# Block compression of a sparse-attention layer: convolution over token pairs in split fp32r, and another order of the dense products

## What is computed

```python
def compress(k_all, pe, w1, w2):
    L = k_all.shape[1]
    n_cmp = (L - CMP_BLOCK) // CMP_STRIDE + 1          # block 32, stride 16
    idx = jnp.arange(n_cmp)[:, None] * CMP_STRIDE + jnp.arange(CMP_BLOCK)[None, :]
    blocks = k_all[:, idx] + pe[None, None, :, None, :]
    hid = jax.nn.gelu(jnp.einsum('bnjgd,jde->bnge', blocks, w1))
    return jnp.einsum('bnge,ef->bngf', hid, w2)
```

## Time and profile before

| | |
|---|---|
| median of 3 runs | 1938.66 us (1932.65 to 1939.78) |
| profiled execution | 1939.67 us, its span 1938.0 us |
| mean granted TensorE clock | 0.918 |
| TensorE / VectorE / ScalarE / GpSimd busy | 1732.1 / 737.3 / 632.9 / 221.3 us |
| compression stage in the trace | 969.8 to 1077.9 us |
| DMA, whole run | 133.47 MB, mean 69 GB/s |

### The profile page before, as it was taken

How to read it: one execution, slowest core, us unless ns; L and a number is a source line. 1 busy time by engine, 2 the same in 40 slices (tenths; PEclk the granted TensorE clock), 3 DMA queues, 4 the chain that set the end, 5 groups by cost and what they waited for, 6 DMA issues and landing times. The chain is left out here.

```text
span 1938.0 us, 31215 instructions
## 1 busy us (share of the span) xinstructions
PE 1732.1 (89%) x12354; PEld 1535.7 (79%) x12354; DVE 737.3 (38%) x1422; ACT 632.9 (33%) x1256; POOL 221.3 (11%) x310
## 2 busy tenths in 40 slices
PE   8994398799999999799779799999697999999996
PEld 7993268699999899699634567767485999998994
DVE  4326953533333222454222354344445333332224
ACT  4425352422222111454112354454314222221113
POOL 1003521200000000100100233232011000000000
PEclk9997698899999999799879679899787999999997
DMA  5322002122222332233452100000321322223321
GB/s 152 90 75 61 22 19 70 44 87 87 87 87 87 90 90 60 44 77 98 113 153 33 44 20 26 1 1 1 110 66 44 87 87 87 87 87 90 90 60 46
DMA packets 257289, 133.47 MB, mean 69 GB/s; under 512 B 47191, under 2 KB 256619, under 8 KB 257003
## 3 DMA queue, kind: packets, MB, share of 16 engines
q1 hardware_dynamic: 247754, 128.44, 23.8%
q10 hardware_dynamic: 8832, 2.20, 0.8%
q0 software_dynamic: 608, 1.57, 0.3%
HBM read 125.88 MB, written 10.43 MB: 70 GB/s over the span
## 5 line engine op out<-in xcount | busy, mean ns | idle before, releaser
L211 PE MATMUL ps<-x_hi,w_hi 128*128 128x272 f32 x2288 | 662.5, 290 | 4.6 <-DVEq L574 4.2
L213 PE MATMUL ps<-x_hi,w_lo 128*128 128x272 f32 x2288 | 664.3, 290 | 0.0
L212 PE MATMUL ps<-x_lo,w_hi 128*128 128x272 f32 x2288 | 659.7, 288 | 0.0
L211 PEld LDWEIGHTS ps<-x_hi,w_hi 128*128 128x128 f32 x2288 | 432.7, 189 | 6.5 <-DVEq L574 4.8
L212 PEld LDWEIGHTS ps<-x_lo,w_hi 128*128 128x128 f32 x2288 | 433.1, 189 | 0.0
L213 PEld LDWEIGHTS ps<-x_hi,w_lo 128*128 128x128 f32 x2288 | 431.8, 189 | 0.0
L226 DVE TENSOR_TENSOR w_lo<-w_raw,w_hi 128x1024 fp32r<-128x1024 f32 (+1 forms) x167 | 226.2, 1355 | 492.5 <-ACT w_hi L219 492.5
L219 ACT ACTIVATE w_hi<-w_raw 128x1024 fp32r<-128x1024 f32 (+1 forms) x179 | 199.6, 1115 | 643.2 <-PE ps L213 636.3
L211 PE MATMUL ps<-h_hi,w_hi 128*128 128x272 f32 x704 | 204.7, 291 | 9.6 <-DVEq L784 9.6
L213 PE MATMUL ps<-h_hi,w_lo 128*128 128x272 f32 x704 | 204.7, 291 | 0.0
L212 PE MATMUL ps<-h_lo,w_hi 128*128 128x272 f32 x704 | 204.4, 290 | 0.0
(11 more groups left out here) (371 smaller groups left out, 2079.2 us busy)
## 6 DMA issues: line engine op xcount, KB each, us to landing
w_raw<-in_ffn_w_gate SPq DMA_DIRECT2D x44, 512.0 KB, 3.9
w_raw<-in_ffn_w_up SPq DMA_DIRECT2D x44, 512.0 KB, 3.9
w_raw<-in_ffn_w_down SPq DMA_DIRECT2D x32, 704.0 KB, 4.6
w_raw<-in_ab_w_in SPq DMA_DIRECT2D x17, 512.0 KB, 4.2
w_raw<-in_c_w_in SPq DMA_DIRECT2D x13, 512.0 KB, 3.8
w_raw<-in_c_w_in SPq DMA_DIRECT2D x16, 256.0 KB, 3.8
w_raw<-in_c_w_out SPq DMA_DIRECT2D x32, 128.0 KB, 3.0
w_raw<-in_ab_w_in SPq DMA_DIRECT2D x10, 256.0 KB, 4.6
```

Of the source, the lines that this page charges most:

```text
L211: pe.matmul(out, c.w_hi[:, slot, k, :], x_hi[:, k0 + k, cols], start=first, stop=False)
L212: pe.matmul(out, c.w_hi[:, slot, k, :], x_lo[:, k0 + k, cols], start=False, stop=False)
L213: last = pe.matmul(out, c.w_lo[:, slot, k, :], x_hi[:, k0 + k, cols], start=False, stop=end)
```

## The change

1. **Token pairs.** A row of the line is now a pair of tokens: partitions are 2 tokens x 64 channels of one head, columns are the pairs, kept in 8 phases (a block is 16 pairs, the stride 8). The DMA brings a pair into one partition: a slot of 128 x 512 holds two pages (64 pairs each), filled by four DMAs of 256-byte pieces. One transpose per head gives the line directly.
2. **Tap halves side by side.** The 128 output columns of a weight tile are taps 0 to 15 and taps 16 to 31 of the same pair position, 64 channels each. One product gives both halves; the second half, shifted by one block, is added afterwards (`shift` on ScalarE, `add` on VectorE). No zeros stand in the weights.
3. **Split fp32r.** Weights and line are split into high and low parts: ScalarE copies, VectorE subtracts. Eight phases x 3 products x 2 column cuts (322 and 320) are 48 matmuls a tag.
4. Weights, position rows and `w2` are loaded by GpSimd in the row stage, with the pairs of the first four sequences; SP loads the other twelve in the compression stage, into 8 slots. Each pair's load reads its page numbers again.
5. The two window copies move into `fetch_values`, at the end of SP's loads in the prompt attention.
6. `pe_unit` goes through both column halves for each row tile.

```diff
 def pe_unit(c, pe, slot, kt, k0, x_hi, x_lo, bank, start, stop):
-    for h in range(2):
-        cols = slice(h * HALF, (h + 1) * HALF)
-        out = c.ps[:, bank + h, 0:HALF]
-        for k in range(kt):
-            first, end = start and k == 0, stop and k == kt - 1
+    halves_of = [(c.ps[:, bank + h, 0:HALF], slice(h * HALF, (h + 1) * HALF)) for h in range(2)]
+    for k in range(kt):
+        first, end = start and k == 0, stop and k == kt - 1
+        for out, cols in halves_of:
             pe.matmul(out, c.w_hi[:, slot, k, :], x_hi[:, k0 + k, cols], start=first, stop=False)
+        for out, cols in halves_of:
             pe.matmul(out, c.w_hi[:, slot, k, :], x_lo[:, k0 + k, cols], start=False, stop=False)
+        for out, cols in halves_of:
             last = pe.matmul(out, c.w_lo[:, slot, k, :], x_hi[:, k0 + k, cols], start=False, stop=end)
...
+def fetch_pair(c, eng, table, step, slot, tags=("k", "v")):
...
+    for g in range(NPAGE):
+        page = page_number(eng, table, b * NPAGE + g, cache)
+        for par in range(2):
+            yield eng.dma_start(slot[HD * g:HD * g + HD, :].rearrange("p (g two e) -> p two g e", two=2, g=4)[:, par],
+                                cache[0][bass.ds(page, 1)].rearrange("a (p two) g e -> p two (a g) e", two=2)[:, par])
...
             @blk.tensor
             def _(pe):
+                pe.transpose(pe_cols, pe_rows[:, :], c.k("ident")[0:2 * PAIRS, 0:2 * PAIRS]).then_inc(pe_t, 1)
                 for tag in range(2):
+                    for n in range(tag * DEC_B, (tag + 1) * DEC_B):
                         if n >= 4:
+                            m = n - 4
+                            pe.wait_ge(line_lo_set, m // DEC_B * n_line + 5 + m % DEC_B + 1)
...
+                        for s in range(2):
+                            for a in range(2):
+                                o, g = (2 * s + a) * P, (2 * a + s) * P
+                                last = pe.transpose(T_BANK(n)[:, o:o + P], slots[n % n_ring][:, g:g + P], c.k("ident"))
                         last.then_inc(turned, 1)
+                    if tag:
                         second(pe, 0)
...
+                    for f in range(PHASES):
+                        at = slice(f * P, (f + 1) * P)
+                        for w, x in ((w_hi, x_hi), (w_hi, x_lo), (w_lo, x_hi)):
+                            for i, (a, b) in enumerate(cuts):
+                                last = pe.matmul(c.ps[:, i, 0:b - a], w[tag][:, at], x[:, f, a:b],
+                                                 start=f == 0 and w is w_hi and x is x_hi, stop=f == PHASES - 1 and w is w_lo)
                     last.then_inc(hid, 1)
...
+                def shift(tag):
+                    act.wait_ge(hid, tag + 1)
...
+                    for i, (a, b) in enumerate(cuts):
+                        copy(h_shift[:, a:b - 1], c.ps[HD:P, i, 1:b - a]).then_inc(shifted, 1)
...
+                for tag in range(2):
+                    w_high(tag)
+                    if tag:
+                        shift(0)
+                    else:
+                        act.wait_ge(pe_t, 1)
+                    copy(pe_of(x_hi), pe_src(tag)).then_inc(line_hi_set, 1)
+                    for s, par in quarters:
+                        copy(prompt_of(x_hi, s, par), prompt_src(tag, s, par)).then_inc(line_hi_set, 1)
+                    for b in range(DEC_B):
+                        n = tag * DEC_B + b
+                        if tag and b == 4:
+                            activate(0)
+                        act.wait_ge(turned, n + 1)
+                        copy(tile_of(x_hi, b), turned_of(n)).then_inc(line_hi_set, 1)
+                    stacks.fill_hi(copy, stacked, tag * n_hi // 2, (tag + 1) * n_hi // 2)
+                shift(1)
+                activate(1)
...
             def fetch_pages(pool, sem):
...
-                for n in range(RING_C):
...
-                pool.wait_ge(landed, 16 * RING_C)
+                raw, _, _ = compress_weights(c)
+                for tag, name in enumerate("kv"):
+                    pool.dma_start(raw[tag].rearrange("p (j e) -> p j e", e=HD), d["c_cmp_w1_" + name][0]
+                                   .rearrange("(j two) d e -> (two d) j e", two=2)).then_inc(landed, 16)
+                for n in range(n_early):
+                    for load in fetch_pair(c, pool, table, (0, n), page_slots[n]):
+                        load.then_inc(landed, 16)
+                zeroed = sem("w2_zeroed")
+                pool.memset(w2d[:, :, :], 0.0).then_inc(zeroed, 1)
+                pool.wait_ge(zeroed, 1)
...
+                pool.wait_ge(landed, 16 * (2 + 4 * n_early + 6))
```

More of the change, by code:

```diff
@@ L1800, in stage_compress @@
+    cuts = [(0, CUT), (CUT, COLS)]
+    h_shift, h_sum = w_raw[0][0:HD, 0:COLS], w_raw[0][HD:P, 0:COLS]
+    n_line = 1 + 4 + DEC_B
     with ExitStack() as tmp:
         sb = lambda n, s, dt=F32: tmp.enter_context(nc.sbuf_tensor(n, s, dt))
[L1802 to L1805, removed]
+        x_hi = sb("cp_line_hi", [P, PHASES, COLS], F32R)
+        x_lo = sb("cp_line_lo", [P, PHASES, COLS], F32R)
@@ new lines, in prompt_src, with pe_of, pe_src, _ @@
+        def prompt_src(tag, s, par):
+            slab = (8, 14)[tag]
+            return projT[rows_of(s), slab:slab + 2, 0:SEQ].rearrange("p a (n f two) -> p two f a n", f=PHASES, two=2)[:, par]
+        def pe_of(x):
+            return x[:, :, PE0:PE0 + 2]
+        def pe_src(tag):
+            return pe_cols[:, tag * PAIRS:(tag + 1) * PAIRS].rearrange("p (h f) -> p f h", h=2)
+        quarters = [(s, par) for s in range(2) for par in range(2)]
+        with block as blk:
+            @blk.sync
+            def _(sp):
+                for n in range(n_early, len(steps)):
+                    if n >= n_ring:
+                        sp.wait_ge(turned, n - n_ring + 1)
+                    for page in fetch_pair(c, sp, table, steps[n], slots[n % n_ring]):
+                        page.then_inc(land[n % n_ring], 16)
@@ L1809, in _ @@
             @blk.gpsimd
             def _(pool):
[L1811 to L1836, removed]
@@ L1873, in _ @@
[L1873 to L1876, removed]
+                    pe.wait_ge(w_lo_set, tag + 1)
+                    pe.wait_ge(line_lo_set, (tag + 1) * n_line)
+                    if tag:
+                        pe.wait_ge(summed, 2)
@@ L1878, in _ @@
                 second(pe, 1)
[L1880 to L1887, removed]
             n_hi, n_lo = len(stacks.hi), len(stacks.lo)
@@ L1925, in _, with w_high @@
-                for tag in range(2):
-                    if tag:
-                        act.wait_ge(hid, 1)
-                    else:
-                        act.wait_ge(zeroed, 3)
-                    load_w1(tag)
-                    if not tag:
-                        for i in range(2):
-                            for s in range(2):
-                                own = rows_of(s)
-                                act.dma_start(w2d[own, i, own], d["c_cmp_w2_" + tags[i]][0]).then_inc(small_in, 16)
-                                act.dma_start(rows[:, i, own], d["c_cmp_pe_" + tags[i]][0]).then_inc(small_in, 16)
-                    place(act, copy, tag, 1)
-                    for n in range(tag * per + 1, (tag + 1) * per, 2):
-                        move(act, copy, n)
-                    stacks.fill_hi(copy, stacked, tag * n_hi // 2, (tag + 1) * n_hi // 2)
-                    act.wait_ge(hid, tag + 1)
-                    copy(bias[:, tag:tag + 1], c.ps[:, 0, N:N + 1]).then_inc(bias_m, 1)
-                    act.wait_ge(bias_m, tag + 1)
+                def w_high(tag):
+                    copy(w_hi[tag].rearrange("p (f h e) -> p f h e", h=2, e=HD), by_phase(w_raw[tag])).then_inc(w_hi_set, 1)
```

134 lines of the change are left out of this document (84 added, 50 removed).

## The result

The changed kernel takes **1890.12 us** (median of 4 runs, 1887.53 to 1896.29) against 1938.84 (median of 4, 1932.65 to 1939.78) for the kernel before beside it: a ratio of 0.976, 95% interval 0.9729 to 0.9791. The forecast was 1907, the range 1882 to 1930.

A forecast was written before the change was run, and what follows sets the result against it. TensorE was taken to bound both convolutions, ScalarE and VectorE the stretch between. Against the profiled 1939.67 us, -46.3 (compression stage) and +13 (row stage) gave -33, so 1907 us; range 1882 to 1930.

The forecast's parts named there:

- the attention's clock: Attention behind the compression stage: up to 18 us either way if another phase wakes the clock earlier or later.
- The bound now: Compression stage before the change: TensorE bounds both convolutions, ScalarE and VectorE the stretch between them.
- Part 1: Convolution: 48 matmuls a tag, 9.2 us with a slow clock start; ends 7.0 (full clock) and 12.8 us.
- Part 2: Feeding the convolutions: SP's issuing decides, 3.3 us a pair (2.8 to 4.0); stage 61.8 us, 46.3 less.
- Part 3: Loads moved to GpSimd in the row stage: +13 us, ends +6 and +31.
- the nearest rival: Row stage: pieces cost GpSimd nothing, issue stays 0.54 us; +6 instead of +13, total 1900 us; 25%.
- the 1900 rival: Row stage: GpSimd's issue stays 0.54 us whatever the size, +6 us, total 1900 us; 25%.
- The slower rival: Row stage: making descriptors on GpSimd costs 11 ns a piece, +78 us, total 1971 us; 11%.
- Part 4: Dense products' new order over 8,976 matmuls: 0 us taken, from -9 to +18.
- the rival at 1 to 2 ns: Dense products: the new order costs 1 to 2 ns a matmul, 9 to 18 us more, total 1920; 5%.
- the one at -12: Dense products: the new order saves up to 12 ns a matmul, 108 us less, total 1800; 5%.
- Part 5: Window copies moved to SP's queue in the prompt attention: cost nothing; without that cover 28 us.

The follow-up runs named there:

- two queues: Changed kernel with every second page pair of the compression stage fetched by GpSimd instead of SP: 1865.69 us, ratio 0.9659.
- the run with the late second product: Changed kernel with odd page pairs fetched by GpSimd, and the keys' GELU and second product moved behind the values' tiles: 1877.99 us, ratio 0.9731.
- the changed kernel's second trace: Changed kernel run again without edit, beside the kernel before: 1899.86 us, ratio 0.9822.
- fillers: Two 512-column products added before each of the attention's first ten wide score tiles: changed kernel 1888.91 us, kernel before 1925.37, changed with odd pairs on GpSimd 1873.38.

## Why the prediction was right, and which terms were off

The sign, the bound and the order of the parts held; the forecast was 17 us too high. Of these, 15 are the attention's clock, 9 the row stage and 5 the dense order, and 12 go the other way, in the stage. The number owes something to luck, twice over. The forecast of -33 is close to the 35 us of the change itself because three misses, +12, -9 and -5, nearly cancel. And the 49 us between the first medians came of a draw: the four runs of before lay at 1932 to 1940 us where later ones went down to 1923.5, and the changed kernel's trace met the short attention.

**The bound now: right.** TensorE bound both convolutions, and with them gone it waits for landed pairs.

**Part 1: right.** 9.2 us a convolution, measured 8.7 and 8.6. The choice was whether it starts slow. TensorE's timeline in the first one, two products to a line:

```profile
995.82 0.73 PE L1917 MATMUL ps<-cp_line_hi,x_hi 128*128 128x322 f32 x2
996.36 0.74 PE L1917 MATMUL ps<-cp_line_lo,x_hi 128*128 128x322 f32 x2
...
999.80 0.47 PE L1917 MATMUL ps<-cp_line_hi,x_lo 128*128 128x322 f32 x2
1000.10 0.46 PE L1917 MATMUL ps<-cp_line_hi,x_hi 128*128 128x322 f32 x2
```

0.27 us a product up to 997.4, the level of 1.2 GHz, then 0.15, that of 2.4 GHz. It rose after some 3.3 us where the earlier trace rows took 4.7, hence 8.7. The Trainium skill's rule ("TensorE: Matmul & The Clock Gate", Part 4) that transposes don't count for the clock as products do agrees with both of these starts, and with the earlier trace rows it doesn't: there the clock rose at 989.8 with nothing but transposes running (0.50 up to 989.7, 1.00 from 989.8), and the first convolution ran at 1.00. With two queues the second convolution ran at 1.00 from its start too, in 7.3 us, near my lower price of 7.0, and in the run with the late second product it started slow and took 10.1. So the rule is no certainty here; both prices occur.

**Part 2: the mechanism right, the size off.** SP decides, as said, and the pair costs 4.3 us, above even my high end of 4.0. The term that was mis-sized is the price of a DMA on SP: I took 0.34 to 0.43 from loads of another shape, though I had 0.6 in Part 3 for the same half-page load on GpSimd; SP takes 0.598. A page number costs about 0.95 where I had 0.74. Twelve pairs by 1.0 us are 12, and the stage was 12.2 longer than forecast. The second convolution starts 56.5 us into the stage, not 43.5. The other terms held: landing 2.3 (2.0), tail 9.0 (9.1). One that I had wrong cost nothing: the four copies of the prompt's columns on ScalarE take 4.4 us, not 2.2, and end long before the pages have landed.

**Part 3: the nearest rival's price.** +4.2, where the flat price gave +6 and I took +13. "Sixteen times the pieces must cost something" was right and small: 0.6 us more for 1,792 more pieces, 0.3 ns each, against the 4.2 ns of my upper bound. The flat 0.54 to 0.58 of the earlier trace rows was the better guide, and the 1900 rival had this term right. The rule of the Trainium skill ("DMA: Bandwidth & Descriptors", Anatomy of one DMA), that many descriptors can be emitted before the incremental cost shows, agrees with these rows up to 256 pieces a DMA (0.60 and 0.62 us); at 2,048 the cost shows, 1.2 us. The slower rival, 11 ns a piece, is excluded by the same row.

**Part 4: nearly right.** The dense order is worth -5 us, inside -9 to +18. A matmul in the new order, which changes bank each time, comes 0.6 ns cheaper; neither the rival at 1 to 2 ns nor the one at -12 holds.

**Part 5: right.** The window copies cost nothing in either place.

**The attention's clock: the bound was right, and it fell on one side.** I had allowed 18 us either way and put half into the range. It gave 14.8. That it fell on the good side was chance: the changed kernel's second trace gave 333.8, 0.8 more than before. My condition ("if another phase wakes the clock") fits the two groups of traces, 6.0 to 6.8 us and 8.2 to 8.5 us behind the fall; that the phase is the cause isn't shown.

## What to carry to other kernels

Price a fetch of small tiles by the DMA and its address arithmetic, on the queue and in the form in which it will be issued, and count them: here 48 DMAs at 0.6 us and their page numbers set the stage once the arithmetic was cheap, and a second issuing engine was worth 20 us of stage, more than half of the 34 that the rewrite had brought there. Before a difference is given to a change, cut both traces at the same events: a third of this gain stood in a stage that nobody had touched, and another execution of the same kernel took it back.

## What was not expected of the hardware

- A half-page load of 256-byte pieces takes 598 ns to issue on SP, the same with 128 and with 256 pieces, and 0.60 and 0.62 us on GpSimd; a weight load of 2,048 pieces takes 1.2 us there. A whole-page load, also with its page number from a register, took SP 0.34. GpSimd's queue made a pair in 3.44 us, SP's in 4.3.
- The attention, the same instructions but for 20 added products in three of the traces, took from 314.8 to 333.8 us over fourteen traces. Its first 40 us stood at a granted clock of 0.50 to 0.52, at 0.67 to 0.75, or with fillers at 0.79 to 0.90; its later 170 us at 1.00 in five and 0.93 to 0.96 in the others. A full clock at its beginning didn't prevent the slow stretch; two added products a tile in its first ten tiles did, in both traces that began 8.2 us or more behind the fall. In the traces with nothing added, 0.50 came where the attention began 8.2 us or more behind the clock's fall, 0.67 or more where it began 6.8 us or less behind it. Why, and what lowers the later part, stays open.
- Row tiles outside and column halves inside, with the bank changing at every matmul and the weights half as often, made a dense fp32r matmul of 272 columns 0.6 ns faster (125.7 to 125.1 ns), in both kernels.
